# Four projection units ahead of their norm, and another order of the products, in a two-block transformer kernel

## The reference

```python
def rms_norm(x, g):                       # rms_norm_2 is the same
    return x * lax.rsqrt(jnp.mean(x * x, axis=-1, keepdims=True) + eps) * g

# end of the first block (f is 4096 -> 1024, the MLP's second product)
h = h + rms_norm(f, norm_mlp_post)

# layer A of the second block; x = h (512 latent tokens), ctx (256 tokens)
hx = rms_norm_2(x, norm_g) * (1.0 + scale_x) + shift_x
hc = rms_norm_2(ctx, norm_g) * (1.0 + scale_c) + shift_c
qx, kx, vx, gx = split(hx @ w_in)         # w_in: 1024 x 4096, 8 heads
qc, kc, vc, gc = split(hc @ w_in)
qx, kx = rope(qx), rope(kx)               # latent tokens alone
s = q . [kc, kx] / 8                      # two maps per head, 64 wide each
a = softmax(s1) - lam * softmax(s2)
o = rms_norm_2(a @ [vc, vx], subln_g) * 0.8 * silu(g)
x = x + gate_x * (ox @ w_o);  ctx = ctx + gate_c * (oc @ w_o)
```

## Time and profile before

| what | value |
|---|---|
| median of three runs | 1629.29 us (1629.29, 1634.57, 1629.10) |
| the profiled execution | 1629.36 us, of which the span is 1627.2 us |
| granted TensorE clock, mean | 0.984 of 2.4 GHz |
| busy: TensorE matmul | 1556.7 us (96%) |
| VectorE / ScalarE / GpSimd | 985.8 (61%) / 751.7 (46%) / 504.6 us (31%) |
| DMA | 149 MB, 92 GB/s in the mean |

### The profile page before, as it was taken

How to read it: one execution, slowest core, us unless ns; L and a number is a source line. 1 busy time by engine, 2 the same in 40 slices (tenths; PEclk the granted TensorE clock), 3 DMA queues, 4 the chain that set the end, 5 groups by cost and what they waited for, 6 DMA issues and landing times.

```text
span 1627.2 us, 23677 instructions
## 1 busy us (share of the span) xinstructions
PE 1556.7 (96%) x8392; PEld 1221.3 (75%) x8392; DVE 985.8 (61%) x2266; ACT 751.7 (46%) x1413; POOL 504.6 (31%) x231
## 2 busy tenths in 40 slices
PE   7998999999899999999899999999999989999997
PEld 5886666678688888888877877778777768876566
DVE  6235555355679867645666666675676267147854
ACT  6225766634342423234344554455445343248753
POOL 3651232245244444444221111121214354230012
PEclk9999999999999999999899999999999989999999
DMA  6861112264356565643111111111111122220001
GB/s 200 174 162 33 59 59 77 76 256 130 104 193 194 191 198 188 198 134 100 53 53 39 40 39 39 39 39 39 39 39 52 52 56 89 78 66 14 2 14 65
DMA packets 48401, 149.34 MB, mean 92 GB/s; under 512 B 5782, under 2 KB 9110, under 8 KB 48184
## 3 DMA queue, kind: packets, MB, share of 16 engines
q1 hardware_dynamic: 37080, 112.45, 23.0%
q10 hardware_dynamic: 11232, 35.72, 6.8%
HBM read 141.53 MB, written 6.62 MB: 91 GB/s over the span
## 4 chain that ended last, share of the span: by engine, by line
PE 80%; DVE 7%; ACT 5%; issue 5%; POOL 1%; DMA 1%; ACTq 0%; POOLq 0%; DVEq 0%; SPq 0%
PE ps L347 41%; PE ps L351 20%; PE ps L570 4%; PE ps L581 3%; PE ps L551 3%; PE ps L1347 3%; PE ps L1311 2%; PE ps L1323 1%; POOL w_l L973 1%; PE ps L415 1%; PE ps L1075 1%; ACT sb L636 1%; DVE tg L1921 1%; ACT w_h L330 1%; DVE b_sb L675 1%
## 5 line engine op out<-in xcount | busy, mean ns | idle before, releaser
L973 POOL TENSOR_TENSOR w_l<-raw,w_h 128x1024 fp32r<-128x1024 f32 (+1 forms) x190 | 457.0, 2406 | 897.1 <-ACT w_h L330 877.4
L330 ACT ACTIVATE w_h<-raw 128x1024 fp32r<-128x1024 f32 x190 | 200.7, 1058 | 360.5 <-PE ps L347 305.3
L347 PE MATMUL ps<-x2h,w_h 128*128 128x512 f32 (+1 forms) x816 | 245.3, 366 | 19.5 <-DVE x2l L1994 7.6
L347 PE MATMUL ps<-x1h,w_h 128*128 128x512 f32 x584 | 237.9, 407 | 16.0 <-POOL w_l L973 10.4
L347 PE MATMUL ps<-x2h,w_l 128*128 128x512 f32 (+1 forms) x816 | 231.8, 349 | 0.0
L351 PE MATMUL ps<-x2l,w_h 128*128 128x512 f32 (+1 forms) x816 | 231.7, 349 | 0.0
L347 PE MATMUL ps<-x1h,w_l 128*128 128x512 f32 x584 | 230.7, 395 | 0.0
L351 PE MATMUL ps<-x1l,w_h 128*128 128x512 f32 x584 | 230.1, 394 | 0.0
L347 PEld LDWEIGHTS ps<-x2h,w_h 128*128 128x128 f32 x816 | 132.4, 191 | 52.6 <-issue 17.1
L347 PEld LDWEIGHTS ps<-x2h,w_l 128*128 128x128 f32 x816 | 132.2, 191 | 20.8
L351 PEld LDWEIGHTS ps<-x2l,w_h 128*128 128x128 f32 x816 | 132.5, 191 | 19.5
(11 more groups left out here) (318 smaller groups left out, 2615.3 us busy)
## 6 DMA issues: line engine op xcount, KB each, us to landing
raw<-in_w_mlp SPq DMA_DIRECT2D x64, 512.0 KB, 3.7
mraw<-in_w_mod ACTq DMA_DIRECT2D x51, 512.0 KB, 3.7
raw<-in_w_a SPq DMA_DIRECT2D x32, 512.0 KB, 3.6
raw<-in_w_att SPq DMA_DIRECT2D x25, 512.0 KB, 11.3
raw<-in_w_b SPq DMA_DIRECT2D x20, 512.0 KB, 3.6
raw<-in_w_g SPq DMA_DIRECT2D x16, 512.0 KB, 3.6
raw<-in_w_ao SPq DMA_DIRECT2D x9, 512.0 KB, 3.5
gates<-g_stage ACTq DMA_DIRECT2D x16, 256.0 KB, 2.2
```

Source lines behind the costliest of these rows:

```text
L330: nc.scalar.activation(split(u)[0], raw[:, u % RAW], ACT.Copy).then_inc(w_hi, 1)
L347: mm = nc.tensor.matmul(o, w[:, k], xh(k), start=(first and k == k0 and wi == 0), stop=(last and k == k1 - 1 and wi == 1))
L973: nc.gpsimd.tensor_tensor(l[:, ks], raw[:, u % RAW, ks], h[:, ks].bitcast(F32), ALU.subtract).then_inc(w_lo, 1)
```

## The change

**Product order.** `products` now finishes the three products of one part before it goes to the next part; on odd k the parts come in reverse order. The products, their number and their sizes are the same.

**The first four units.** For units 0 to 3 of layer A, TensorE multiplies latent tiles that are not yet normalised: `xph`, `xpl` hold the high and low half of hc (1 + scale) g. Since the factor 1/rms belongs to a token, it is applied behind the product: VectorE multiplies the PSUM bank by rstd (`evict_first`). The shift belongs to a feature, so its product with the weights is a constant for each output column: two more columns (`mod`'s shift, one is used) are appended to the context part, which becomes 258 columns wide, and the result `shifted` is added by ScalarE as a bias (`take_first`). All later units use `x2h` and `x2l` as before; these are now made while units 2 and 3 are multiplied.

**Around it.** TensorE does parts of the context products of unit 0 between the column sums and the spread of the first norm. A column sum of the second norm and the latent products of units 0 and 1 alternate tile by tile. Unit 2 and 3 are done in parts. Unit 2 has a split slot of its own (`w_h4`, `w_l4`), and ScalarE splits it as soon as the MLP is over. VectorE rotates q, does the gate, then rotates k. In head 0 (`lead`), nine tiles of head 1 come ahead of the scores, and the other calls of `dense` are shorter, so that it is 32 tiles again. ScalarE takes q of head 1 behind the first rotation, ahead of the exponentials. The rest of the edit makes room in SBUF (rows of `x2h` are four columns longer) and unrolls GpSimd's first four splits.

```diff
+THIRD = {... U_A + 2: 3}                     # unit 2 splits into w_h4, w_l4
@@ products
-                for wi, w in enumerate(split(u)):
-                    for o, xh, xl in parts:
-                        mm = nc.tensor.matmul(o, w[:, k], xh(k), ...)
-                    if wi == 0:
-                        for o, xh, xl in parts:
-                            mm = nc.tensor.matmul(o, w[:, k], xl(k), start=False, stop=False)
+                w_hu, w_lu = split(u)
+                for o, xh, xl in parts if k % 2 == 0 else parts[::-1]:
+                    nc.tensor.matmul(o, w_hu[:, k], xh(k), ...)
+                    nc.tensor.matmul(o, w_hu[:, k], xl(k), start=False, stop=False)
+                    mm = nc.tensor.matmul(o, w_lu[:, k], xh(k), ...)
@@ TensorE
             nm3a.wait(pe, "add", KT - 1)
             column_sums(sqsum, 4, S, True, False)
+            pe.wait_ge(ml_f, 4 + N_MLP - 2)
+            first_ctx(0, 1, 0, 2)
             nm3a.wait(pe, "sq", KT)
             column_sums(sq[:, 1], 4, S, False, True).then_inc(nm3a.mm, 1)
+            first_ctx(0, 1, 2, 4)
             nm3a.wait(pe, "rc", 1)
             nm3c.wait(pe, "lo", KT)
             spread(5, 0, 4).then_inc(nm3a.r, 1)
-            first_ctx(0, 0, KT)
-            tile_sum(0)
-            first_ctx(1, 0, KT // 2)
-            tile_sum(1)
-            first_ctx(1, KT // 2, KT)
-            for k in range(2, KT):
-                tile_sum(k)
+            first_ctx(0, 1, 4, KT)
+            pe.wait_ge(ml_f, 4 + N_MLP)
+            first_ctx(1, 3, 0, KT)
+            for k in range(KT):
+                tile_sum(k)
+                nm3p.wait(pe, "lo", k + 1)
+                for j in range(2):
+                    mm = first_x(j, 2 * j, k, k + 1)       # xph, xpl
+                    ...
+            first_x(2, 4, 0, 4)
             nm3b.wait(pe, "rc", 1)
             spread(7, 0, 4).then_inc(nm3b.r, 1)
-            for k in range(KT + LAG):
-                ...                                        # first_x of units 0 and 1
+            first_x(2, 4, 4, KT)
+            nm3b.wait(pe, "src", KT)
+            first_ctx(2, 5, 0, KT).then_inc(unit, 1)
+            first_ctx(3, 6, 0, KT)
+            wait_head(pe, "k", (None, 0), 1, 1)
+            first_x(3, 2, 0, KT).then_inc(unit, 1)
@@ TensorE, attend
+                lead = i is None and c == 0
+                if lead:
+                    dense(9)
+                    wait_head(pe, "g", head, 1, 1)
                 wait_head(pe, "ro", head, 2, 2)
                 scores(0)
-                dense(2 if more else 3)
+                dense(1 if lead else 2 if more else 3)
...
-            project((None, 0), 2 * KT, 2 * KT)
@@ ScalarE
             mlp(3, False, True)
+            split_high(act, U_A + 2)
...
             for k in range(KT):
                 nm3b.wait(act, "src", k + 1)
+                nc.scalar.activation(xph[:, k, :], hc[:, k, 0:S], ACT.Copy, scale=mulx[:, 0, 0, k:k + 1]).then_inc(nm3p.hi, 1)
...
+            nc.scalar.activation(rstd[:, 0:S], ps[:, 7], ACT.Copy).then_inc(n3_r, 1)
+            split_high(act, U_A + 3)
+            def take_first(j, dst, scale):
+                wait_head(act, "em", (None, 0), 8, 2 * j + 2)
+                nc.scalar.activation(dst[:, S:SC], ps[:, 2 * j + 1, 0:C], ACT.Copy, scale=scale)
+                return nc.scalar.activation(dst[:, 0:S], ps[:, 2 * j], ACT.Identity, bias=shifted[:, j:j + 1], scale=scale)
@@ VectorE
+            def g_low(k):
+                nm3p.wait(v, "hi", k + 1)
+                nc.vector.scalar_tensor_tensor(out=xpl[:, k, :], in0=hc[:, k, 0:S], scalar=mulx[:, 0, 0, k:k + 1],
+                                               in1=xph[:, k, :].bitcast(F32), op0=ALU.mult, op1=ALU.subtract).then_inc(nm3p.lo, 1)
...
+            def evict_first(j, bank, ctx_bank, scale):
+                unit_done(v, U_A + j)
+                nc.vector.tensor_scalar(shifted[:, j:j + 1], ps[:, ctx_bank, C:C + 1], scale, None, ALU.mult).then_inc(ha["em"], 1)
+                nc.vector.tensor_tensor(ps[:, bank], ps[:, bank], rstd[:, 0:S], ALU.mult).then_inc(ha["em"], 1)
             invert(v, nm3b, S)
-            modulated(nm3b, 0, xn3, (0,))
+            evict_first(0, 0, 1, -0.125)
+            evict_first(1, 2, 3, 1.0)
+            modulated(nm3b, 0, xn2, (0,))
+            evict_first(2, 4, 5, 1.0)
+            ...                                            # the same for unit 3
```

More of the change, by code:

```diff
@@ L307, in split @@
                 return w_h3[:], w_l3[:]
+            if THIRD.get(u) == 3:
+                return w_h4[:], w_l4[:]
             if u >= N_ATT:
@@ L327, in split_high @@
                     act.wait_ge(up_free, 4)
+            elif i is None and u == U_A + 2:
+                act.wait_ge(unit, U_A)
             else:
@@ L439, in build @@
         nm3a = Norm(**none, add=KT - 1)
+        nm3p = Norm(src=0, sq=0, add=0, mm=0, ln=0, rc=0, r=0, t=0)
         nm3b = Norm(add=0, mm=0)
@@ L995, in _ @@
                     low(U_MLP + j, i, 16)
-            lows(U_A, U_AO + 1)
+            for u in range(U_A, U_A + 4):
+                low(u)
+            lows(U_A + 4, U_AO + 1)
             g.wait_ge(ha["lo"], KT - 2)
@@ L1590, in take @@
                 unit_done(act, U_A + 4 * c + j, i, 8)
-                begins = i is None and c == 0
-                src = pair(j if begins and j < 3 else 0)[:, 0:SC]
-                if begins and j < 3:
-                    split_high(act, U_A + j + 2)
+                src = pair(0)[:, 0:SC]
                 if j == 0:
@@ L1602, in take @@
                     nc.scalar.activation(a_g[c % 2][:], src, ACT.Tanh, scale=0.5).then_inc(ha["gt"], 1)
-                if ahead and (j == 3 or not begins):
+                if ahead:
                     split_high(act, U_A + 4 * c + j + 2, i, 8)
@@ L1653, in attend @@
                         high(k)
+                lead = i is None and c == 0
+                if lead:
+                    wait_head(act, "ro", head, 2, 1)
+                    take((None, 1), 0, True)
                 if c:
@@ L1663, in attend @@
                 exps(1, 1)
-                if more:
+                if more and not lead:
                     take((i, c + 1), 0, True)
-                else:
+                elif not more:
                     take_out(0)
@@ L1688, in attend @@
                     take_out(6)
-            for j in range(4):
-                take((None, 0), j, True)
             all_heads(act, attend)
@@ L2014, in mlp @@
                             nm3c.wait(v, "r", 1)
+                            done(nc.vector.tensor_copy(x2h[:, :, SC:SC + 2], mod[:, 0:KT, :]))
+                            settle(v)
+                            done(nc.vector.tensor_tensor(x2l[:, :, SC:SC + 2], mod[:, 0:KT, :],
+                                                         x2h[:, :, SC:SC + 2].bitcast(F32), ALU.subtract))
+                            settle(v)
                         x_tile(k, 0, xn3, 1).then_inc(nm3c.t, 1)
```

140 lines of the change are left out of this document (87 added, 53 removed).

## The result

The changed kernel took 1640.80 us in the median of five runs (1639.17 to 1641.40), the kernel before 1629.29 beside it; the ratio is 1.0055, with a 95% interval of 1.0040 to 1.0071: 9 us slower (6.5 to 11.6). The forecast was 1625, with a range from 1618.5 to 1631.5. The profiled execution took 1639.17 us, its span 1637.1 instead of 1627.2.

The account below looks back on a forecast made before the run. TensorE's own work plus its few waits was taken as the bound (busy 96%). Gains of 2.4 us from the stretch to head 1 and 1.7 from product order, 4.1 together, took 1629.3 to 1625.2; range 1618.5 to 1631.5.

Parts of the forecast that it names:

- (5): Ahead of head 0's scores: eight leading tiles of head 1 run to 841.8; the ninth waits for the first rotation.
- (1): First norm: 12 context matmuls fill gaps around two column sums; the spread moves from 791.35 to 791.75, 0.4 us lost.
- (2): First norm: clock stays at 2.4 GHz, the spread takes half its 1.86 us, 36 context matmuls end at 797.1.
- (3): Units 0 and 1: TensorE sets the pace, 2.31 us a tile against VectorE's 2.05; eight tiles from 797.2 to 815.7.
- (4): Units 2 and 3, done in parts: all four first units are done at 833.4 instead of 846.0.
- (6): VectorE's chain from second spread through both rotations, meeting GpSimd's splits, ends at 850.3: head 0's scores 4.3 us later.
- rival D: VectorE's chain from second spread to second rotation is longer than forecast, head 0's scores after 855: 1632 us; chance 0.13.
- (7): Head 0 with 23 tiles takes 43.8 us, plus 0.5 for a_k; head 1's scores at 894.6, 4.7 us gained.
- (8): Wait ahead of head 0's scores: clock falls to half speed for 4.7 us, costing 2.3; 2.4 us gain remains.
- The product order: In products, 312 tiles: half of them slow and half their 22 ns excess saved by the new order, 1.7 us gained.

Follow-up runs that it names:

- e1_late_ones: The changed kernel with TensorE's wait for ones_r moved from ahead of head 0 to behind its nine leading tiles; 1630.68 us, ratio 0.9994 to the kernel before.
- e7_all: e1_late_ones with ScalarE's splits of units 3 to 5 moved, rows of 3136 bytes, old product order, head 1's k taken earlier; 1626.93 us, ratio 0.9967.
- e11_keep_clock: e7_all with 18 more products of 512 columns behind the ninth leading tile, into a bank nobody reads; 1626.22 us, ratio 0.9958 to the kernel before.

## Why the prediction was wrong

The step that failed is (5): "Eight run to 841.8." I took the first eight leading tiles as free to run as soon as unit 3 was done. Ahead of all heads the program has a wait of TensorE for `ones_r`. In the kernel before, the first thing behind it was the scores, which wait for the second rotation anyway, so it cost nothing. The change puts nine tiles into the head and leaves the wait in front of them. The order of instructions had said so: in the rows of the order quoted with the change, the scores of the kernel before wait for `ha_ones`, and those of the changed one do not. The name had moved to the first leading tile, a row that I did not quote. I had looked at the ninth tile's waits and not at the first one's, and had no rival in which the leading tiles come too late to fill anything.

By its own steps:

- (1) The spread at 791.89 in place of 791.75, with 0.33 us of wait where 0.87 stood: right.
- (2) The clock at 1.00 through 820, the last context product at 797.2 (797.1 forecast): right.
- (3), (4) The first of the eight column sums at 797.25, unit 2's context columns at 821.98, unit 3 done at 833.2, against 797.2, 822.2, 833.4: right. VectorE had 2.05 us a tile, TensorE 2.28. The forecast called a matmul of one column 119 ns; it leaves two records of 119 ns, so that is half of it. No term hung on this, since the 0.95 us of a whole column sum is a row.
- (5) Failed, as said: 848.98 instead of 833.4 for the first leading tile.
- (6) VectorE's rotations ended at 848.8 instead of 850.3: the collisions were 2.11 us on a low tile, which I had put into rival D, and 2.82 in the first rotation; the second one met none here, though it did in e1_late_ones (2.55), as forecast. The first collision speaks for the Trainium skill (SBUF — State Buffer, "Who interferes with whom"), which says that a VectorE instruction with two SBUF inputs contends with a GpSimd instruction that reads SBUF, and that the port pair they share is an exclusive lock: the scalar_tensor_tensor at 829.10 reads two SBUF tiles, and took 2.11 us in place of 0.75 where the split of unit 4 ran.
- (7), (8) can be read only where the wait is gone. In e1_late_ones the scores stand 62.96 us behind the first column sum (62.6 forecast), and head 1's transposes of v 2.5 us earlier than before (2.4 forecast). Part of this agreement is luck: TensorE waited 2.31 us for `a_k` in head 0 where 0.5 was allowed, and three waits of the old head 0, 1.5 us together, were gone. The clock was back 4.5 us behind the scores in e1_late_ones (4.7 forecast); its part was put at 2.3 us and measured 2.7 in e7_all against e11_keep_clock, where it was low for 6.5 us behind them.
- The product order: 1.7 us forecast, 0 or a small loss measured. Here the rule of the Trainium skill (TensorE: Matmul & The Clock Gate, "Back-to-back issue gap"), that load and matmul together set the spacing, was the better guide: each weight load stands behind one matmul in either order, and the order gained nothing that the runs can tell.
- Not in the sum: 1.2 us from the last head to the first scores of layer B. 0.8 of it stands where the 512-column products have the slower pace, so it comes from where the tiles lie; I had taken the longer rows as room in SBUF and nothing else. The rest lies round a norm with a low clock, a stretch that takes 31.8 to 34.1 us in the thirteen profiles, so it can't be put down to the change.

The measured parts add up: 1629.3 + 8.0 + 1.2 + about 0.6 at the end = 1639.1, where the profiled execution took 1639.17. Without the wait (e1_late_ones) the stretch term was right to 0.1 us, with the luck named above, and the ratio of 0.9994 agrees, within its interval, with 2.5 us gained less what layer B and the last spread gave back.

Rival D, the slow side at 0.13, had its mechanism in VectorE's chain, and that chain was shorter than forecast. No case of mine had TensorE idle from 833 on, and so none reached 1640.

## What to carry to other kernels

When work is moved ahead of a point in a hand-written queue, read every wait that stands between its new place and the instruction before it, also those outside the function that the edit touches: a wait that cost nothing in front of an instruction that was late anyway becomes the whole cost of what is now put behind it. In an order of instructions with their waits, compare the waits of the first moved instruction, not of the last. And a gap that is to be filled with other work should be filled whole: nine tiles left 4.5 us and a clock at half speed behind them, twelve left 1.5 us and the full clock.
